# Score pairs behind quarters of the tiles, one block for piece, turn and swap, and the w_ada pieces requested on ScalarE's queue

## The reference

```python
mod = jnp.dot(jax.nn.silu(c), w_ada) + b_ada
shift, scale, gate = jnp.split(mod, 3, axis=-1)
h = rmsnorm(x, g) * (1 + scale[:, None]) + shift[:, None]
xa, za, qb, kb, vb, zb, qc, kc, vc, zc, qi, ki, wi = project(h, w_i)
...
hs = rglru(causal_conv(xpad, cw, cb), h0, wrg, brg, wig, big, lam)
...
qi, ki = rope_partial(qi, pos), rope_partial(ki, pos)
sc = jnp.einsum('thd,sd->ths', qi, ki) * IDX_DIM ** -0.5
score = jnp.einsum('ths,th->ts', jax.nn.relu(sc), w)
vals, idx = lax.top_k(score, topk)
...
return x + gate * out
```

## Time and profile before

| | |
|---|---|
| median of three runs | 2551.24 us |
| profiled execution | 2549.4 us, span 2547.3 us |
| mean granted TensorE clock, of full speed | 0.955 |
| TensorE busy (PE) | 2350.7 us |
| weight loads (PEld, beside PE) | 2172.0 us |
| VectorE (DVE), ScalarE (ACT), GpSimd (POOL) busy | 981.1, 807.2, 854.2 us |
| read from HBM, written | 280.81 MB, 30.92 MB |
| quarters of weights on SP's queue | 448 and 128 of 256 KB, landing in 2.9 and 2.8 us |
| halves of pieces on SP's queue | 64 of 1024 KB, landing in 7.7 us |

### The profile page before, as it was taken

How to read it: one execution, slowest core, us unless ns; L and a number is a source line. 1 busy time by engine, 2 the same in 40 slices (tenths; PEclk the granted TensorE clock), 3 DMA queues, 4 the chain that set the end, 5 groups by cost and what they waited for, 6 DMA issues and landing times.

```text
span 2547.3 us, 46977 instructions
## 1 busy us (share of the span) xinstructions
PE 2350.7 (92%) x18247; PEld 2172.0 (85%) x18247; DVE 981.1 (39%) x1900; ACT 807.2 (32%) x1543; POOL 854.2 (34%) x651
## 2 busy tenths in 40 slices
PE   4589999999999999988994999999999999997997
PEld 2267888889999998977993888999999999986997
DVE  7433355554311223443117234777511122353113
ACT  0122333334333333342222233445333333333221
POOL 5122223323333333333442322344433333343441
PEclk6589999999999999998996999999999999998999
DMA  8955555664333332223441554333333333222443
GB/s 284 357 188 172 157 160 178 181 199 127 96 88 91 90 80 76 77 59 116 131 119 39 164 150 122 80 82 79 93 90 92 92 81 84 76 74 79 129 130 137
DMA packets 442877, 312.07 MB, mean 123 GB/s; under 512 B 21304, under 2 KB 413376, under 8 KB 441480
## 3 DMA queue, kind: packets, MB, share of 16 engines
q1 hardware_dynamic: 415064, 283.35, 37.8%
q10 hardware_dynamic: 27632, 26.21, 3.3%
HBM read 280.81 MB, written 30.92 MB: 122 GB/s over the span
## 4 chain that ended last, share of the span: by engine, by line
PE 69%; issue 15%; POOL 5%; DMA 4%; DVE 4%; DVEq 1%; ACT 1%; ACTq 0%; SPq 0%; POOLq 0%
PE proj L606 20%; PE proj L608 20%; PE proj L612 19%; POOL w_lo L501 4%; PE misc L803 2%; PE misc L776 2%; DMA rel_windows<-rel_rows 1%; PE proj L654 1%; PE misc L785 1%; DMA work<-in_w_ada 1%; DMA x_keep<-xy 1%; PE misc L734 1%; POOL act_lo L494 1%; PE proj L624 1%; DVE act_lo L1273 1%
## 5 line engine op out<-in xcount | busy, mean ns | idle before, releaser
L606 PE MATMUL proj<-act_hi,w_hi 128*128 128x288 f32 (+1 forms) x4672 | 1342.1, 302 | 65.4 <-issue 33.8
L608 PE MATMUL proj<-act_lo,w_hi 128*128 128x288 f32 (+1 forms) x4672 | 1317.1, 297 | 0.0
L501 POOL TENSOR_TENSOR w_lo<-raw,w_hi 128x512 fp32r<-128x512 f32 (+1 forms) x584 | 763.3, 1309 | 1471.7 <-ACT w_hi L975 1471.7
L612 PE MATMUL proj<-act_hi,w_lo 128*128 128x288 f32 (+1 forms) x4672 | 1004.1, 296 | 0.0
L606 PEld LDWEIGHTS proj<-act_hi,w_hi 128*128 128x128 f32 (+1 forms) x4672 | 885.0, 189 | 108.9 <-issue 93.6
L608 PEld LDWEIGHTS proj<-act_lo,w_hi 128*128 128x128 f32 (+1 forms) x4672 | 886.1, 190 | 2.1
L612 PEld LDWEIGHTS proj<-act_hi,w_lo 128*128 128x128 f32 (+1 forms) x4672 | 755.3, 189 | 0.0
L975 ACT ACTIVATE w_hi<-raw 128x512 fp32r<-128x512 f32 (+1 forms) x584 | 364.4, 629 | 1183.3 <-PE proj L612 1165.1
L1276 DVE SCALAR_TENSOR_TENSOR acc<-work,kw_tok,acc 128x256 f32<-128x256 f32 (+3 forms) x128 | 72.9, 600 | 131.6 <-ACT work L1040 125.5
L1276 DVE SCALAR_TENSOR_TENSOR xy<-misc,hg,xy 128x512 f32<-128x512 f32 (+1 forms) x32 | 16.6, 517 | 243.1 <-PE misc L803 242.7
L1276 DVE SCALAR_TENSOR_TENSOR xy<-proj,mod,lb 128x224 f32 (+5 forms) x72 | 25.6, 412 | 209.4 <-PE proj L612 209.4
(11 more groups left out here) (192 smaller groups left out, 1743.3 us busy)
## 6 DMA issues: line engine op xcount, KB each, us to landing
raw<-in_w_in SPq DMA_DIRECT2D x448, 256.0 KB, 2.9
xy<-in_w_ada SPq DMA_DIRECT2D x64, 1024.0 KB, 7.7
work<-in_w_ada SPq DMA_DIRECT2D x32, 1024.0 KB, 10.9
raw<-in_w_out SPq DMA_DIRECT2D x128, 256.0 KB, 2.8
x_keep<-xy ACTq DMA_DIRECT2D x32, 288.0 KB, 2.5
lb<-x_keep SPq DMA_DIRECT2D x24, 288.0 KB, 3.2
x_keep<-xy ACTq DMA_DIRECT2D x4, 1152.0 KB, 15.4
out_y_prompt<-work SPq DMA_DIRECT2D x4, 1024.0 KB, 4.1
```

The lines of the kernel that those rows point to most:

```text
L501: pool.tensor_tensor(w_lo[:, c, :, 0:width], raw[:, c, :, 0:width], w_hi[:, c, :, 0:width].bitcast(F32), ALU.subtract)\
L606: pe.matmul(dst, w_hi[:, c, kk, 0:width], act_hi[:, k, cols], start=(k == 0), stop=False)
L608: pe.matmul(dst, w_hi[:, c, kk, 0:width], act_lo[:, k, cols], start=False, stop=False)
L612: m = pe.matmul(proj[b][0:width, half, 0:HALF], w_lo[:, c, kk, 0:width], act_hi[:, k, cols], start=False, stop=(k == KT - 1))
```

## The change

On TensorE the score group is split into its four pairs. Pairs 3 and 4 of query q-2 stand behind quarters 0 and 1 of query tile q, pairs 1 and 2 of query q-1 behind quarters 2 and 3. Between quarters 1 and 2 stand both halves of the piece, the turn, and the swap, which now also waits for late_read; in the recurrent tiles both halves and the turn stand together behind the second quarter. The last pairs (3 and 4 of query 6, all of query 7) move into the first two recurrent tiles, and the wait for ScalarE behind the last scores into block 1. ScalarE has the relus by pairs between its copies of weights, and requests the pieces on its own queue, each behind the copy of a tile's last quarter (third quarter in the query tiles); SP requests none. VectorE takes the rows of a piece ahead of the rotary, adds the scores by pairs, and frees the bank behind the rotary's first operation, with a drain.

```diff
-            def load_late(l, i):
-
-                layer, col = (l, 2 * D_MODEL + AW * i) if i < AT else (l + 1, AW * (i - AT))
-                w = inp["w_ada"][layer].rearrange("(k p) n -> p k n", p=P)
-                n = LATE_AT[l] + i
-                if i == 0:
-                    hold(sp, h_low_g, (l * 2 * KT + KT) // 2)
-                    hold(sp, h_low_v, (l * 2 * KT + KT) // 2)
-                for u in range(2):
-                    if n > 0:
-                        hold(sp, late_used, 2 * n + u - 1)
-                    sp.dma_start(late_w[:, u], w[:, u * 8:u * 8 + 8, col:col + AW]).then_inc(late_in[u], 16)
-
...
-                    if q > 0:
-                        load_late(l, q - 1)
...
-                    if AT + 2 * g - 1 < LATE[l]:
-                        load_late(l, AT + 2 * g - 1)
-                    elif g == 0:
-                        load_late(l, AT - 1)
...
-                def late(i, u, b):
-
-                    if u == 1 and 0 < i <= LATE[l]:
+                def late(i, b):
+
+                    if i < LATE[l]:
+                        late_unit(i, 0, b)
+                        late_unit(i, 1, b)
+                    if 0 < i <= LATE[l]:
                         late_turn(i - 1, b)
-                    if i < LATE[l]:
-                        late_unit(i, u, b)
...
-                def scores(q, first=False):
+                def score(q, b, first=False):
 
                     hold(pe, roped, l * 17 + q + 2)
-                    for e, (b, hh) in enumerate((b, hh) for b in (1, 2, 3, 4) for hh in range(2)):
+                    for hh in range(2):
+                        e = 2 * (b - 1) + hh
                         hold(pe, idx_read, l * 64 + (8 * q + e - 3 if not first or e > 3 else 0))
...
                 def query_tile(q, b, use, first=False):
 
-                    chunks(QI + q, b, use, (0, 1))
+                    chunks(QI + q, b, use, (0,))
+                    if not first:
+                        score(q - 2, 3, q == 2)
+                    chunks(QI + q, b, use, (1,))
+                    if not first:
+                        score(q - 2, 4, q == 2)
+                    late(q, b)
+                    hold(pe, late_read, LATE_AT[l] + q + l)
                     swap(QI - 1 + q, 1 - b, swap_i[:, :], qi_raw, P)
-                    late(q, 0, b)
                     chunks(QI + q, b, use, (2,))
-                    late(q, 1, b)
-                    chunks(QI + q, b, use, (3,))
                     if first:
                         hold(pe, ki_ready, l + 1)
                         hold(pe, t_read, l * T_EV + 2)
-                    scores(q - 1, first)
+                    score(q - 1, 1, first)
+                    chunks(QI + q, b, use, (3,))
+                    score(q - 1, 2, first)
...
                     if g == 1 and LATE[l] == AT:
                         hold(pe, late_read, LATE_AT[l] + AT + l + 1)
-                    chunks(LRU + 2 * g, 1, g + 4, (0,))
-                    if not first:
-                        gates(g - 1)
-                    chunks(LRU + 2 * g, 1, g + 4, (1,))
                     if first:
+                        chunks(LRU, 1, 4, (0,))
+                        score(6, 3)
+                        chunks(LRU, 1, 4, (1,))
+                        score(6, 4)
+                        late(AT, 1)
+                        hold(pe, late_read, LATE_AT[l] + AT + l)
                         swap(QI + 7, 0, swap_i[:, :], qi_raw, P)
-                    late(AT + 2 * g, 0, 1)
-                    chunks(LRU + 2 * g, 1, g + 4, (2,))
-                    late(AT + 2 * g, 1, 1)
-                    chunks(LRU + 2 * g, 1, g + 4, (3,))
-                    if first:
-                        scores(7)
+                        chunks(LRU, 1, 4, (2,))
+                        score(7, 1)
+                        chunks(LRU, 1, 4, (3,))
+                        score(7, 2)
+                        chunks(LRU + 1, 0, 5, (0,))
+                        score(7, 3)
+                        chunks(LRU + 1, 0, 5, (1,))
+                        score(7, 4)
+                        late(AT + 1, 0)
+                        chunks(LRU + 1, 0, 5, (2, 3))
+                        return
+                    if g == 1:
                         hold(pe, idx_read, (l + 1) * 64)
                         t_event(2)
+                        if LATE[l] == AT:
+                            hold(pe, late_read, LATE_AT[l] + AT + l + 1)
+                    chunks(LRU + 2 * g, 1, g + 4, (0,))
+                    gates(g - 1)
+                    chunks(LRU + 2 * g, 1, g + 4, (1,))
+                    late(AT + 2 * g, 1)
+                    chunks(LRU + 2 * g, 1, g + 4, (2, 3))
                     chunks(LRU + 1 + 2 * g, 0, g + 5, (0, 1))
-                    late(AT + 1 + 2 * g, 0, 0)
-                    chunks(LRU + 1 + 2 * g, 0, g + 5, (2,))
-                    late(AT + 1 + 2 * g, 1, 0)
-                    chunks(LRU + 1 + 2 * g, 0, g + 5, (3,))
+                    late(AT + 1 + 2 * g, 0)
+                    chunks(LRU + 1 + 2 * g, 0, g + 5, (2, 3))
...
+            def load_late(l, i):
+
+                if i >= LATE[l]:
+                    return
+                layer, col = (l, 2 * D_MODEL + AW * i) if i < AT else (l + 1, AW * (i - AT))
+                w = inp["w_ada"][layer].rearrange("(k p) n -> p k n", p=P)
+                n = LATE_AT[l] + i
+                if i == 0:
+                    hold(act, h_low_g, (l * 2 * KT + KT) // 2)
+                    hold(act, h_low_v, (l * 2 * KT + KT) // 2)
+                for u in range(2):
+                    if n > 0:
+                        hold(act, late_used, 2 * n + u - 1)
+                    act.dma_start(late_w[:, u], w[:, u * 8:u * 8 + 8, col:col + AW]).then_inc(late_in[u], 16)
...
                 def query_tile(q, b, first=False):
-                    upper(QI + 1 + q, range(4))
+                    upper(QI + 1 + q, (0,))
+                    if not first:
+                        relus(q - 2, 3, q == 2)
+                    upper(QI + 1 + q, (1,))
+                    if not first:
+                        relus(q - 2, 4, q == 2)
+                    upper(QI + 1 + q, (2,))
+                    load_late(l, q + 1)
+                    relus(q - 1, 1, first)
+                    upper(QI + 1 + q, (3,))
                     take_query(q, b)
-                    relus(q - 1, first)
+                    relus(q - 1, 2, first)
...
+                        upper(LRU + 1, (0,))
+                        relus(6, 3)
+                        upper(LRU + 1, (1,))
+                        relus(6, 4)
+                        upper(LRU + 1, (2,))
+                        load_late(l, AT + 1)
+                        relus(7, 1)
+                        upper(LRU + 1, (3,))
+                        take_input(0)
+                        relus(7, 2)
+                        upper(LRU + 2, (0,))
+                        relus(7, 3)
+                        upper(LRU + 2, (1,))
+                        relus(7, 4)
+                        upper(LRU + 2, (2, 3))
+                        load_late(l, AT + 2)
+                    else:
+                        upper(LRU + 1 + 2 * g, (0, 1))
                         gates(g - 1)
-                    upper(LRU + 1 + 2 * g, (2, 3))
-                    take_input(g)
-                    if first:
-                        relus(7)
-                    upper(LRU + 2 + 2 * g, (0, 1))
-                    if not first:
+                        upper(LRU + 1 + 2 * g, (2, 3))
+                        load_late(l, AT + 1 + 2 * g)
+                        take_input(g)
+                        upper(LRU + 2 + 2 * g, (0, 1))
                         square_states(g - 1)
-                    upper(LRU + 2 + 2 * g, (2, 3))
+                        upper(LRU + 2 + 2 * g, (2, 3))
+                        load_late(l, AT + 2 + 2 * g)
...
-                def rotate(n, raw_parts, rot, b, kept=False):
+                def rotate(n, raw_parts, rot, b):
 
                     hold(dve, swapped, l * 17 + n + 1)
                     rows = rot.shape[0]
                     tt(halves(rot), wide(proj[b])[0:rows], halves(rope[0:rows, 1, :]), ALU.mult)
-                    if not kept:
-                        dve.drain().then_inc(bank_free[b], 1)
+                    dve.drain().then_inc(bank_free[b], 1)
...
+                def take_rows(q, b):
+
+                    hold(dve, evac, l * OUT + QI + q + 1)
+                    late_take(q, b)
...
-                    late_take(q, b)
-                    dve.drain().then_inc(bank_free[b], 1)
...
+                for q in range(8):
+                    take_rows(q, (q + 1) % 2)
+                    if q > 0:
+                        add_scores(q - 1, 3)
+                        add_scores(q - 1, 4)
+                    query(q, (q + 1) % 2, q == 0)
+                    add_scores(q, 1)
+                    add_scores(q, 2)
```

(67 more changed lines are left out.)

## The result

The changed kernel takes 2584.26 us, the median of four runs (2576.98 to 2590.02), against 2550.61 before: a ratio of 1.013 (95% interval 1.0103 to 1.0156), some 34 us slower. Forecast was 2550.6, with a range of 2541 to 2563. The profiled execution took 2590.0 us (span 2588.2), 40.6 us more than the one of before.

The account below looks back on a forecast made before the run. TensorE's own stream was taken as the bound, busy 2350.7 of 2549.4 us. Terms -4.6 - 3.4 - 1.5 + 3 + 5.9 = -0.6, applied to the median 2551.24, gave 2550.6 us, range 2541 to 2563.

Parts of the forecast that it names:

- the pieces in the recurrent tiles: Layer 0: earlier requests but raw chunks cutting in, second half late; +0.45 us a pair, seven pairs, +3 us (-10 to +20).
- nothing is to be won from the clock: Six query tiles of layer 0 ran at a granted clock of 1.00, so the clock offered no gain there.
- slower by landings: Rival: second half lands 1 us later in all seven pairs, +13, 2563 us; 0.27 shared with rotary and unchanged tiles.
- A new wait at the first gates: Second recurrent tile: moved score pairs delay VectorE's convolution; TensorE waits 1.6 us in layer 0, 4.3 in layer 1: +5.9.
- First pieces: Pieces 0 and 1 of each layer: asked for some 2 us earlier, both halves needed at once; -1.5 us (-4 to +3).
- Query tiles: q = 2 to 7, both layers: score waits go, one cut comes; 20.15 against 20.53 us a tile, -4.6 us in all.
- The groups of queries 0 and 7: Both layers: end wait goes, two groups gain 0.7 each, added cuts cost some; -3.4 us (-5 to 0).
- the edit does not do what it says: Rival: score pairs still wait for ScalarE, query tiles stay at 20.5, 2558.6 us; 0.27 shared with slower by landings and rotary.

Follow-up runs that it names:

- experiment 9: The changed kernel with only a quarter of each raw chunk requested in layer 0's recurrent tiles from block 1 on: 2553.32 us, ratio 0.9999 to the kernel before.
- experiment 1: The changed kernel with the halves of a piece apart again in the recurrent tiles, still requested on ScalarE's queue: 2537.23 us, ratio 0.9961 to the kernel before.
- experiment 3: The changed kernel with halves apart in the recurrent tiles and pieces requested on SyncE's queue: 2589.61 us, ratio 1.0165 to the kernel before.
- experiment 4: The kernel before with pieces requested on ScalarE's queue, halves apart and scores in one group: 2534.85 us, ratio 0.9951 to the kernel before.

## Why the prediction was wrong

**The step that failed: the pieces in the recurrent tiles, +3 us forecast, +28.4 measured.** "A wait of 2.2 instead of 1.76" in the odd tile, +0.45 a pair. The mechanism was named: requests 2.3 us earlier, raw chunks cutting in, a wait within the piece at its second half. Two sizes failed. The DMA issue of the second half of piece 13 (its own us to landing last), which answers to the 8.0 of the earlier trace rows:

```profile
xy<-in_w_ada ACTq DMA_DIRECT2D x1, 1024.0 KB, 9.6
```

It was issued 0.4 behind the first, so it landed 10.0 us behind that, not 9.3, and the stops of the odd tiles were 2.3 to 2.9 us. What cut in was under-counted. Between the first request and the second landing, the queues of ScalarE (q10) and SyncE (q1) in the changed kernel, and SyncE's in the same stretch of before, moved (packets, MB, share):

```profile
q10 hardware_dynamic: 2080, 2.10, 65.2%
q1 hardware_dynamic: 1670, 0.83, 31.6%
```

```profile
q1 hardware_dynamic: 3157, 2.64, 98.6%
```

(In the kernel before, q1 carries the halves too.) The halves are 2.10 MB and a raw chunk 0.26. So 3.2 chunks went beside the halves, where the forecast has two, and 2.1 in the 8.55 us of before, where it has one.

And I gave the stops no price beyond their length. The forecast says that nothing is to be won from the clock, from a row of query tiles; that is no row of the stretch in which waits were to grow. The trace of before had a sign: its odd tiles stop for 1.7 to 1.9 us, at 1.00, but piece 23 stopped it for 2.88 us, and that tile has a clock of 0.84 and is 20.97 us long, 3.7 more than the others. By that row seven odd tiles with such a stop would have cost some 26 us more (an estimate). It was no sure sign: piece 1 stopped TensorE for 2.42 us, and that tile has 1.00:

```profile
185.35:208.35 23.00, 20.00 (x187) 16.86 (x185) 4.61 (x8) 8.57 (x19) 6.37 (x5) 1.00 0.50 149
```

With the stop as short as forecast the price might have stayed away: in experiment 9 stops of up to 2.2 us left the clock at 1.00. The two sizes failed together. The rival "slower by landings" had the place and the direction, and its condition was met (a landing over 9.8 us behind the issue); it priced waits alone, 2563.

The Trainium skill, TensorE: Matmul & The Clock Gate, section "HAM oscillation — how this bites in real kernels", describes this pattern: each wait for data is followed by matmuls at half rate, paid at every tile. The trace agrees in part: 0.50 in three windows behind the 2.89 us, but 1.00 behind the 2.42 of the earlier trace rows, so not each wait is paid for. On the queues, the Trainium skill, DMA: Bandwidth & Descriptors, "Queues, rings and completion order", as cited in the forecast, held: with a quarter of each raw chunk beside it (experiment 9) the second half landed after some 8.0 us, and after 9.6 with all of it.

**A new wait at the first gates, +5.9.** The waits were 3.19 and 4.61 us, against 1.6 and 4.3 forecast. Layer 1, TensorE:

```profile
1640.80 2.27 PE L717 MATMUL misc<-work,w_rg 128*128 128x290 f32 x4 [4.61 <-issue]
```

Right in place and chain; in layer 0 one copy on VectorE ahead of the convolution took 1.27 us where it takes 0.17 in layer 1, for a reason that stays open. But the tiles lost 4.8 and 7.6 us, 12.4 in all: the clock again (0.92 and 0.85 in them).

**First pieces, -1.5.** Query tiles 0 and 1 lost 1.2 us in layer 0 and 5.5 in layer 1; the clock was 0.86 in query tile 1 of layer 0 and 0.79 in query tile 0 of layer 1. The earlier request didn't help piece 0 of layer 1: its halves, among raw chunks, landed 9.65 and 13.54 us behind their issues (6.38 and 8.93 before), 10.0 and 14.4 us into the tile, later than before.

**Query tiles, -4.6.** Right in direction and too small: 19.87 us a tile, -8.1 us in all (3.95 in layer 0, 4.14 in layer 1). Quarters (13.48) and scores (3.23) came as taken; the block of pieces, turn and swap took 3.16 us instead of 3.4. No wait appeared in it.

**The groups of queries 0 and 7, -3.4.** Can't be read alone: query tile 1 holds both this and a stopped piece. The tiles LRU and LRU+1, which hold the other part, changed by -0.3 and +0.4 us.

In the order query tiles, first pieces, recurrent tiles, gates, LRU and LRU+1, these sum to -8.1 + 6.7 + 28.4 + 12.4 + 0.1 = 39.5 of the 40.6 us between the two profiled executions. The rival "the edit does not do what it says" was wrong: no score waits for ScalarE in the query tiles.

## What to carry to other kernels

Price a stop of TensorE by its length and by the granted clock of the stretch behind it, and look for stops of that length in the trace you have before you call it cheap. Where they went both ways, as here, the slow stretch belongs in the range. Parts of a transfer that land one after the other should be consumed with work between them: joining two small consumers into one block saved 0.3 us of cuts a tile and cost up to 6 (an odd tile of 21.42 us against 15.45 in experiment 1). A request moved to an earlier queue is worth its head start less what the other queue moves meanwhile.

## What was not expected of the hardware

The length of a stop did not decide whether the clock fell. The first gates of layer 0 stopped TensorE for 3.19 us in the changed kernel and for 3.18 us in experiment 9. The same tile in the two:

```profile
366.38:388.54 22.16, 18.98 (x175) 17.31 (x174) 13.63 (x32) 9.33 (x12) 5.42 (x4) 0.92 0.50 149
```

```profile
364.81:385.36 20.55, 17.37 (x175) 16.27 (x173) 13.63 (x32) 9.33 (x12) 5.41 (x4) 1.00 0.40 123
```

In experiment 3 stops of 1.87 and 1.91 us were followed by a tile clock of 0.91, and others of 1.86 to 1.99 by 1.00. What decides is not shown by these runs.

The same output tile (O+7, 96 matmuls and the ends of its neighbours) at a granted clock of 1.00 took 12.64 us in layer 0 and 12.48 us in layer 1 of the kernel before, and 12.90 in layer 1 of experiment 4:

```profile
1234.16:1246.80 12.64, 12.64 (x99) 12.64 (x98) 1.82 (x4) 3.21 (x5) 5.16 (x4) 1.00 0.44 130
...
2407.78:2420.26 12.48, 12.48 (x98) 12.48 (x97) 1.83 (x4) 3.23 (x5) 5.19 (x4) 1.00 0.44 131
```

```profile
2397.50:2410.40 12.90, 12.90 (x98) 12.90 (x97) 1.83 (x4) 3.21 (x5) 5.18 (x4) 1.00 0.42 127
```

The changed kernel's had 12.64 in both layers. So the pace differs between layers of one execution as well as between executions, by up to some 5 us over the 13 tiles O+2 to O+14 of a layer; its cause is open.
